# One copy of 127 shifted rows becomes a copy of 112 rows and a copy of 15 rows

## The reference

```python
proj = rmsnorm(x, norm_mix_g) @ w_in                     # 1792 columns for group A, 1024 for group B
prev_rows = concatenate([shift_prev[:, None, :], pa[:, :-1]], axis=1)   # pa = proj[..., :1792]
xm = pa + (prev_rows - pa) * mu                          # token shift
...                                                      # RWKV-7 recurrence on xm, gMLP gating on the rest
x = x + concatenate([A, B]) @ w_out
x = x + peer_ffn(rmsnorm(x, norm_ffn_g))                 # 128 gathered expert rows of U and of V per token
x = x + (p @ ple_w) * sigmoid(rmsnorm(x, norm_ple_g) @ ple_gate_w)
```

## Time and profile before

| what | us |
|---|---|
| median of 3 runs (4623.56 to 4630.86) | 4624.03 |
| the profiled execution's own time | 4615.67 |
| its span in the trace | 4613.9 |

### The profile page before, as it was taken

How to read it: one execution, slowest core, us unless ns; L and a number is a source line. 1 busy time by engine, 2 the same in 40 slices (tenths; PEclk the granted TensorE clock), 3 DMA queues, 4 the chain that set the end, 5 groups by cost and what they waited for, 6 DMA issues and landing times.

```text
span 4613.9 us, 42693 instructions
## 1 busy us (share of the span) xinstructions
PE 3585.8 (78%) x14690; PEld 2207.8 (48%) x14690; DVE 2542.9 (55%) x5603; ACT 899.5 (19%) x2202; POOL 2343.3 (51%) x2110
## 2 busy tenths in 40 slices
PE   4745987599868998599858998599866988857757
PEld 3733564356534654356534654356533654323414
DVE  1561748275836575275826575275735666365732
ACT  1210312032112112032112112031112112111112
POOL 1011746276646656375636656375545755454641
PEclk8877998799988999799988999799988999988878
DMA  7135889699987999789977899789986999979964
GB/s 224 49 107 201 328 319 331 223 362 348 381 297 276 341 379 358 257 306 345 366 282 279 331 385 359 257 305 334 359 289 254 345 383 347 344 263 346 371 255 170
DMA packets 554196, 1390.59 MB, mean 301 GB/s; under 512 B 39913, under 2 KB 274697, under 8 KB 553986
## 3 DMA queue, kind: packets, MB, share of 16 engines
q0 software_dynamic: 297216, 1082.26, 63.1%
q1 hardware_dynamic: 256770, 305.61, 19.5%
HBM read 1366.88 MB, written 13.56 MB: 299 GB/s over the span
## 4 chain that ended last, share of the span: by engine, by line
PE 53%; DMA 20%; DVE 17%; issue 4%; ACT 3%; SPq 2%; POOL 1%; DVEq 0%; PEldq 0%; ACTq 0%
PE peer_acc L718 23%; PE bank L737 11%; DMA wbuf<-in_w_in_dram 7%; PE bank L842 6%; PE bank L819 5%; DMA proj_s<-pa 5%; DMA wbuf<-in_peer_wq_dram 4%; DVE uring L1220 4%; PE bank L686 2%; DVE feat L1412 1%; DMA wbuf<-in_w_out_dram 1%; SPq L375 1%; DVE feat L1409 1%; DVE e L1415 1%; PE bank L930 1%
## 5 line engine op out<-in xcount | busy, mean ns | idle before, releaser
L718 PE MATMUL peer_acc<-vring,dg 128*128 128x512 f32 x4096 | 1963.3, 622 | 233.1 <-ACT dg L1013 156.6
L657 POOL DMA_INDIRECT vring<-in_peer_v_dram,eidx x1024 | 1147.8, 1121 | 1501.4 <-PE peer_acc L718 1295.0
L647 POOL DMA_INDIRECT uring<-in_peer_u_dram,eidx x1024 | 1168.0, 1141 | 683.9 <-issue 308.5
L718 PEld LDWEIGHTS peer_acc<-vring,dg 128*128 128x128 f32 x4096 | 767.4, 198 | 1105.2 <-issue 911.4
L1220 DVE CUSTOM_DVE_ANT_0 uring<-uring,px 128x1024 f32<-128x1024 f32 x1024 | 1226.6, 1220 | 36.1 <-DMA uring<-in_peer_u_dram,eidx 16.9
L737 PE MATMUL bank<-wbuf,xT 128*128 128x256 f32 (+1 forms) x2288 | 568.6, 406 | 386.7 <-DMA wbuf<-in_w_in_dram 369.0
L737 PEld LDWEIGHTS bank<-wbuf,xT 128*128 128x128 f32 (+1 forms) x2288 | 430.3, 190 | 569.1 <-issue 478.3
L1013 ACT ACTIVATE dg<-ident,qa 128x128 f32<-128x128 f32 x1024 | 325.3, 389 | 644.0 <-DVE qa L1225 628.0
L1225 DVE TENSOR_TENSOR qa<-qg,pgate 128x4 f32<-128x4 f32 x256 | 40.4, 158 | 613.5 <-ACT qg L1017 613.4
L819 PEld LDWEIGHTS bank<-xT,wbuf 128*128 128x128 f32 x2048 | 258.6, 206 | 80.6 <-issue 76.6
L819 PE MATMUL bank<-xT,wbuf 128*128 128x128 f32 (+1 forms) x2048 | 261.0, 287 | 45.3 <-DMA wbuf<-in_peer_wq_dram 41.7
(11 more groups left out here) (321 smaller groups left out, 3431.5 us busy)
## 6 DMA issues: line engine op xcount, KB each, us to landing
wbuf<-in_w_in_dram SPq DMA_DIRECT2D x91, 1024.0 KB, 10.6
wbuf<-in_peer_wq_dram SPq DMA_DIRECT2D x64, 1024.0 KB, 13.4
wbuf<-in_w_out_dram SPq DMA_DIRECT2D x32, 1024.0 KB, 8.3
wbuf<-in_ple_gate_w_dram SPq DMA_DIRECT2D x20, 1024.0 KB, 10.0
uring<-in_peer_u_dram,eidx POOLq DMA_INDIRECT x1024, 6.8
vring<-in_peer_v_dram,eidx POOLq DMA_INDIRECT x1024, 6.7
feat<-in_shift_mu_dram SPq DMA_DIRECT2D x9, 896.0 KB, 27.1
xm<-pa SPq DMA_DIRECT2D x8, 889.0 KB
```

Of the source, the lines that this page charges most:

```text
L647: gp.indirect_dma_start(uring[:, c % NU, :], None, peer_u, bass.IndirectOffsetOnAxis(ap=eidx[:, i % 2, k:k + 1], axis=0)).then_inc(sig(f"u ...
L657: gp.indirect_dma_start(vring[:, c % NV, :], None, peer_v, bass.IndirectOffsetOnAxis(ap=eidx[:, i % 2, k:k + 1], axis=0)).then_inc(sig(f"v ...
L718: last = mm(acc[half][:, :], dg[:, (c // UNIT) % 2, c % UNIT, :], vring[:, c % NV, half * 512:(half + 1) * 512], start=(c % HK == 0), stop ...
```

## The change

The copy at L468 is issued as two DMAs, one of the first 112 rows and one of the 15 rows behind them. Both add to the same semaphore, so the count that VectorE waits for rises from 32 to 48 for each prompt block.

```diff
+SPLIT = 112
...
                     at = lambda k: proj_s[k:k + 1, :]
-                    sp.dma_start(xm[1:P, :], pa[0:P - 1, :]).then_inc(sig("prev_loaded"), 16)
+                    sp.dma_start(xm[1:SPLIT + 1, :], pa[0:SPLIT, :]).then_inc(sig("prev_loaded"), 16)
+                    sp.dma_start(xm[SPLIT + 1:P, :], pa[SPLIT:P - 1, :]).then_inc(sig("prev_loaded"), 16)
                     sp.dma_start(at(i + 1), pa[P - 1:P, :]).then_inc(sig("proj_stored"), 16)
...
                 yield "shift0"
-                ve.wait_ge(sig("prev_loaded"), 32 * i + (32 if prompt else 16))
+                ve.wait_ge(sig("prev_loaded"), 48 * i + (48 if prompt else 16))
```

## The result

The changed kernel takes 4357.24 us (median of 4 runs, 4355.35 to 4374.17) against 4627.03 us for the kernel before, runs of which were added on the same chip. The ratio is 0.9425, with a 95% interval of 0.94 to 0.945. The profiled execution took 4355.35 us, 260.3 us less than the profiled one of before. Forecast were 4318 us, in a range of 4270 to 4390: the direction and the place were right, the gain was 270 us where 306 were forecast.

What follows compares the result with a forecast made beforehand. The prediction took the 127-row copy on one DMA engine, holding up SyncE's queue and `win9`, as the bound. Gains of 272 us (fronts 1 to 7) and 34 (front 0) off 4615.67, plus 8.4 to the median, gave 4318 us, range 4270 to 4390.

Steps and rivals of the forecast that it cites:

- One engine: The 127-row copy runs on one DMA engine of sixteen, share 0.06 at some 26 GB/s; 112 rows were taken to spread.
- Fronts 1 to 7: TensorE's gap at `win9` behind the copy: 6 us kept of the mean 44.9, so 7 x 38.9 = 272 us gained.
- The sign that the wait for `win9` is under 10 us in each front: In the profile after, TensorE's wait for the weight load `win9` was to be under 10 us in each front.
- Front 0: VectorE's first shift starts near 68 with the copy spread, the first gathers follow: 34 us gained, 28 if factors land slower.
- The sum: Whole kernel: 272 + 34 = 306 us off the profiled 4615.67, so 4309.7; with 8.4 us for the runs' median, 4318.
- Hidden issues: SyncE's one more issue in eight fronts, 0.65 us by the median, is hidden in fronts 1 to 7.
- Given back to the gathers: Rival: behind the gap, catching up runs slower and only 25 us are gained per front, so 4415; chance 0.06.
- Slow store: Rival: the row store to DRAM takes its 30 us by itself, gaps stay, 4629 to 4646; chance 0.03.
- not spread: Rival: the 112-row copy stays on one engine and all gaps stay, 4629, no change; chance 0.03.

Runs made afterwards that it cites:

- second profile of the changed kernel: The changed kernel (112 + 15 rows) run once more, with nothing altered, against the kernel before: 4365.16 us, ratio 0.944; its profiled execution took 4368.21 us.
- second profile of before: The kernel before, run and profiled once more with nothing altered: 4624.71 us; its first profiled execution took 4615.67 us.

## Why the prediction was right, and where its sizes were off

**One engine.** Right, and shown: 127 and 113 rows give a share of 0.06 at 26 GB/s, 122 rows 0.12 at 51, 112 rows none of it. That the row store was only a victim is shown by the run with 127 rows in ScalarE's queue: its issue went from 30.63 to 0.38 us, and the time stayed.

**Fronts 1 to 7.** This term was mis-sized. The prediction kept 6 us of each gap, with 0 and 15 as the ends; the chip keeps 12.6 (88.2 / 7), near the far end, and 10.5 (73.7 / 7) in the second profile of the changed kernel. The sign that the wait for `win9` is under 10 us in each front failed in all seven (10.0 to 15.4). The gain is 309.4 - 88.2 = 221 us against the second profile of before, 226 against the first, and not 272. The step that failed is that the load of `win9` lands in the median time, or in 21 us at worst, with the copy and the factors counted as plain bytes. It lands 24 us after its issue in front 2. What stands ahead of it in the queue is the cause: moved behind `win9`, copy and factors hold up `win10` by as much, and with the copy in ScalarE's queue `win9` is on time and `win7` or `win8` is late instead. The spread copy itself is dear, about 200 GB/s where I had counted with 300 and more. How the 12.6 us divide between copy, factors and gathers isn't settled: each remedy takes away a part, and together they don't add up.

**Front 0.** 34 us were predicted. The first shift starts 29.9 us earlier, for the same reason. By the first gather, which starts at 296.05 in place of 317.64, only 21.6 seem gained. That goes with the one profile that I had: in it the clock was still 1.00 at 200 us, in the second profile of before it had fallen to 0.50 as in the profiles after, and the first gather started at 326.50. Against that, 30.5 us are gained.

**The sum.** Against the second profile of before: 30.5 + 221.2 = 251.7 of 4624.71 - 4355.35 = 269.4 us. 17.7 us are left. With the second profile of the changed kernel the same sum is 31.2 + 235.7 = 266.9 of 4624.71 - 4368.21 = 256.5 us, 10.4 too many. What is left changes its sign from one execution to the next, so no further term of the change is shown.

**Hidden issues.** Right: the stage ends at 796.3, before `win7` is used. **Given back to the gathers.** This rival didn't come in: from `win9` in front 2 to `win9` in front 3 it takes 461.9 us (826.89 to 1288.83) in place of 492.7 (906.47 to 1399.18), 30.8 us less, and the gap of front 3 is shorter by 30.7 (14.00, 44.67). The same holds for the other five such stretches, 31.1 to 43.5 us less with gaps shorter by 31.2 to 36.9. Nothing is given back behind the gaps. **Slow store, not spread:** both excluded, by the 0.41 us and by the windows.

## What to carry to other kernels

A window in which the DMA share is 1 over the number of engines, behind a transfer of some hundred KB, says that this transfer runs on one engine; look at its row count before anything else. The chain and the waits name what stands behind such a transfer (here a store of 7 KB and a weight load), not the transfer itself. Splitting pays only if the parts have row counts that spread, and what is then still in front of the next urgent load is worth trying in another engine's queue: 112 and 15 rows issued by ScalarE had the lowest ratio here of the versions that leave nothing out, 0.9345 against 0.9425, though other loads then waited. For a copy on one engine that change of queue gave nothing (1.0).

## What the runs showed of the hardware that was not expected

A copy from SBUF to SBUF that keeps all engines busy moves far less than sixteen times what one engine moves: one engine alone went at 26 GB/s and two at 51, but with all of them the windows show 201 to 229 GB/s at a share of about 1. The factors aren't the reason, as the 201 and 202 were read without them; no run here tells what is.

A copy from another engine's queue can hold up a load that was handed over before it: `win8`, issued just ahead of the 127 rows in both kernels, came 20.6 us late in front 2 with the copy in ScalarE's queue, and at most 1.6 us late with the copy behind it in SyncE's own.

And the granted clock of TensorE can fall to half in one execution of a kernel and not in another, at about the same place and with the engine busy in both. With the fall the first gather started 8.9 us later (326.50 against 317.64), nearly all of the 9.0 us between the two profiled executions of before (4615.67 and 4624.71).
